# A ring of twelve weight slots in place of six for the experts of a two-block network on one Trainium2 core

## The reference, cut to what matters

```python
def moe_ffn(h, w_router, b_router, w_gate_up, b_gate_up, w_down, b_down):   # h: 256 x 1024
    logits = h @ w_router + b_router
    top_val, top_idx = lax.top_k(logits, 4)          # 4 of 32 experts for each token
    gates = jax.nn.softmax(top_val, axis=-1)
    ...
    def expert_block(args):
        xe, e = args
        gu = xe @ w_gate_up[e] + b_gate_up[e]        # 1024 x 2048
        g = jnp.minimum(gu[:, :1024], 7.0)
        u = jnp.clip(gu[:, 1024:], -7.0, 7.0)
        act = (u + 1.0) * (g * jax.nn.sigmoid(1.702 * g))
        return act @ w_down[e] + b_down[e]           # 1024 x 1024
    ...                                              # times its gate, summed over each token's experts
```

## Time and profile before

| | |
|---|---|
| Median of 3 runs | 2454.33 us (2451.05 to 2455.43) |
| The profiled execution, its own time | 2454.55 us |
| Its span, first to last instruction | 2452.9 us |
| TensorE busy, share of the span | 2257.8 us, 92% |
| VectorE, ScalarE, GpSimd busy | 1003.7, 623.0, 168.7 us |
| Bytes moved by DMA | 633.59 MB, mean 258 GB/s |
| Experts phase, from its first DMA (1438.97) to the last copy out of PSUM | about 998 us |

### The profile page before, as it was taken

How to read it: one execution, slowest core, us unless ns; L and a number is a source line. 1 busy time by engine, 2 the same in 40 slices (tenths; PEclk the granted TensorE clock), 3 DMA queues, 4 the chain that set the end, 5 groups by cost and what they waited for, 6 DMA issues and landing times. The chain is left out here.

```text
span 2452.9 us, 32053 instructions
## 1 busy us (share of the span) xinstructions
PE 2257.8 (92%) x12673; PEld 1398.2 (57%) x12674; DVE 1003.7 (41%) x1460; ACT 623.0 (25%) x848; POOL 168.7 (7%) x192
## 2 busy tenths in 40 slices
PE   7999989899999999989989989999999999999996
PEld 5886775688778777658868644333333333333332
DVE  4553582664466437556548641111111111111111
ACT  3432331443433322243426510000000000000000
POOL 4000020000000002000000000000000000000000
PEclk9999999999999999999999979999999999999999
DMA  8762312676287242158625349999999999999996
GB/s 281 260 234 79 112 64 69 230 255 219 72 301 243 73 158 78 37 181 279 227 82 161 117 165 371 418 418 418 418 418 411 404 404 411 407 405 399 404 403 248
DMA packets 231951, 633.59 MB, mean 258 GB/s; under 512 B 32472, under 2 KB 128744, under 8 KB 199056
## 3 DMA queue, kind: packets, MB, share of 16 engines
q1 hardware_dynamic: 231856, 632.24, 68.4%
HBM read 631.12 MB, written 1.07 MB: 258 GB/s over the span
## 5 line engine op out<-in xcount | busy, mean ns | idle before, releaser
L2511 PE MATMUL banks<-memory,attend_words 128*64 128x512 f32 x2048 | 481.1, 605 | 63.2 <-DMA memory<-in_w_gate_up 62.3
L365 PE MATMUL banks<-ffn_room 128*128 128x512 f32 x1920 | 454.4, 392 | 0.0
L365 PEld LDWEIGHTS banks<-ffn_room 128*128 128x128 f32 x1920 | 357.5, 188 | 73.6
L2511 PEld LDWEIGHTS banks<-memory,attend_words 128*64 128x64 f32 x2048 | 131.1, 136 | 388.1 <-issue 210.6
L2661 DVE TENSOR_TENSOR attend_words<-banks,memory 64x512 f32<-64x512 f32 x64 | 44.2, 690 | 738.4 <-PE banks L2511 738.0
L485 DVE TENSOR_TENSOR ffn_room<-memory,ffn_room 128x2048 fp32r<-128x2048 f32 x124 | 281.0, 2291 | 122.0 <-ACT ffn_room L442 122.0
L396 PE MATMUL banks<-ffn_room 128*128 128x512 f32 x1056 | 254.2, 397 | 17.4 <-DVE ffn_room L522 17.4
L442 ACT CAST ffn_room<-memory 128x2048 fp32r<-128x2048 f32 x124 | 232.7, 1906 | 106.9 <-PE banks L396 82.7
L396 PEld LDWEIGHTS banks<-ffn_room 128*128 128x128 f32 x1056 | 201.8, 192 | 66.2 <-DVE ffn_room L522 20.3
L2527 PE MATMUL banks<-memory,attend_words 128*64 128x512 f32 x1024 | 226.8, 594 | 0.0
L2527 PEld LDWEIGHTS banks<-memory,attend_words 128*64 128x64 f32 x1024 | 70.0, 135 | 130.9 <-issue 119.9
(11 more groups left out here) (419 smaller groups left out, 2108.4 us busy)
## 6 DMA issues: line engine op xcount, KB each, us to landing
memory<-in_w_gate_up SPq DMA_DIRECT2D x256, 1024.0 KB, 11.8
memory<-in_ffn_w SPq DMA_DIRECT2D x132, 1024.0 KB, 6.9
memory<-in_w_down SPq DMA_DIRECT2D x128, 1024.0 KB, 13.0
memory<-in_w_in SPq DMA_DIRECT2D x32, 1024.0 KB, 5.4
memory<-in_w_ada SPq DMA_DIRECT2D x32, 768.0 KB, 5.8
memory<-in_w_out SPq DMA_DIRECT2D x12, 1024.0 KB, 5.1
memory<-in_w_in SPq DMA_DIRECT2D x8, 800.0 KB, 4.6
memory<-in_ln_g SPq DMA_DIRECT2D x6, 512.0 KB, 3.9
```

Source lines behind the costliest of these rows:

```text
L365: m = nc.tensor.matmul(psum[:, GU + tt, :], x_parts[:, xp, k, tt * P:tt * P + P], rows, start=(n == 0), stop=(n == 3 * KD - 1))
L2511: m = mm(psum[halves[h], bank, :], room.xeT[:, k, :], rows[:, c0 + h * HALF:c0 + h * HALF + HALF], start=(k == 0), stop=(k == G8 - 1))
```

## The change

The ring's six slots stay as they are for all phases. For the experts six more places are added, each with a semaphore of its own (`chip.more`): slots 2 to 5 of `attend_later`, a new piece of `attend_words` (SLOT words more in `ATTEND_WORDS`), and `chip.xT`, which attention itself uses. Five of these (all but `chip.xT`) are loaded in the attention phase, right behind `b_down` on SP and ahead of the last four loads into the ring: chunks 6 and 7 of expert 0 and 0, 1, 2 of expert 1. The sixth place is loaded as the first load of the experts phase. From there on, each expert's 12 chunks have 12 fixed places, and a load waits for the chunk that was 12 before it in place of 6.

```diff
@@ class Chip
         *self.full, self.used = semaphores(nc, "ring", RING + 1)
+        self.more = semaphores(nc, "more", RING)
@@ class AttendRoom
         self.gatesT = w.take(chip.T)
+        self.more = [later[:, i * SLOT:i * SLOT + SLOT] for i in range(2, 6)] + [w.take(SLOT), chip.xT.rearrange("p k t -> p (k t)")]
@@ attend_phase, SP
             sp.dma_start(room.b_down[0:NE, :], b_down[0:1, :, :].rearrange("a e n -> (a e) n")).then_inc(s["mod"], 16)
+            for m in range(RING, 2 * RING - 1):
+                dst = room.more[m - RING]
+                sp.dma_start(dst, gate_up_rows(w_gate_up, *divmod(m, KD))).then_inc(chip.more[m - RING], 16)
             chip.issue(sp, loads, OUT + RING, OUT + N_OUT + RING)
@@ experts_phase
-    assert LOADS % RING == 0
+    CYCLE = 2 * RING
+    assert LOADS == CYCLE and CYCLE - G8 == D4
+    def place(e, j):
+        return j if first_turn(e) else (G8 + j) % CYCLE
     def slot(e, j):
-        return chip.slot(base + (j if first_turn(e) else G8 + j))
+        p = place(e, j)
+        return chip.ring[:, chip.slot(base + p), :] if p < RING else room.more[p - RING]
@@ experts_phase, SP
             def load(e, j, src):
-                sp.wait_ge(chip.used, taken(e, j - RING + 1))
+                sp.wait_ge(chip.used, taken(e, j - CYCLE + 1))
...
             def turn(e):
                 bias_row(e)
-                for k in range(G8):
-                    load(e, k, gu_rows(e, k))
+                for k in range(0 if not isinstance(e, int) else D4, G8):
+                    load(e, k, gate_up_rows(w_gate_up, e, k))
                 for k in range(D4):
                     load(e, G8 + k, down_rows(e - 1, k))
             bias_row(0)
-            for k in range(RING, G8):
-                load(0, k, gu_rows(0, k))
+            load(1, D4 - 1, gate_up_rows(w_gate_up, 1, D4 - 1))
             turn(1)
             with sp.Fori(2, NE) as e:
                 turn(e)
```

More of the change, by code:

```diff
@@ L1556, with gate_up_rows @@
 ALL = 2 * STEPS
+def gate_up_rows(w_gate_up, e, k):
+    return w_gate_up[0:1, ds1(e), k * P:k * P + P, :].rearrange("a e p n -> (a e p) n")
 def attend_loads(chip, w_in, w_out):
@@ L1604, in __init__, with attend_phase @@
         self.rows_rms = acc[:, 4 * WIDE:4 * WIDE + chip.T]
-ATTEND_WORDS = 6144 + 256 + 3 * WIDE + 4 * WIDE + 2048 + 4 * HD + P + 32 + 192 + 8 * NE + 2 * NE + 2 * P + 4 + 24 + 10 * NE
+ATTEND_WORDS = 6144 + 256 + SLOT + 3 * WIDE + 4 * WIDE + 2048 + 4 * HD + P + 32 + 192 + 8 * NE + 2 * NE + 2 * P + 4 + 24 + 10 * NE
 PIECES = ((0, P), (P, WIDE))
-def attend_phase(chip, s, routed, room, par, loads, base, n_project, b_down, mod_row):
+def attend_phase(chip, s, routed, room, par, loads, base, n_project, b_down, mod_row, w_gate_up):
     nc, D, KD, NT = chip.nc, chip.D, chip.KD, chip.NT
@@ L2390, with __init__ @@
 class ExpertRoom:
-    def __init__(self, chip, words):
+    def __init__(self, chip, words, attend):
+        self.more = attend.more
         w = Words(words, 0, EXPERT_WORDS)
@@ L2437, in slot, with filled @@
     def slot(e, j):
-        return chip.slot(base + (j if first_turn(e) else G8 + j))
+        p = place(e, j)
+        return chip.ring[:, chip.slot(base + p), :] if p < RING else room.more[p - RING]
     def full(e, j):
-        if first_turn(e):
-            return 16 * ((base + j) // RING + 1)
-        return e * (16 * LOADS // RING) + 16 * ((base + G8 + j) // RING + 1 - LOADS // RING)
+        p = place(e, j)
+        return chip.full[chip.slot(base + p)] if p < RING else chip.more[p - RING]
+    def filled(e, j):
+        p = place(e, j)
+        first = 16 * ((base + p) // RING + 1) if p < RING else 16
+        return first if first_turn(e) else e * 16 + (first + 16 * ((G8 + j) // CYCLE - 1))
     halves = [slice(CAP * h, CAP * h + CAP) for h in range(2)]
@@ L2461, in load @@
             def load(e, j, src):
-                sp.wait_ge(chip.used, taken(e, j - RING + 1))
-                dst = chip.ring[:, slot(e, j), :]
+                sp.wait_ge(chip.used, taken(e, j - CYCLE + 1))
+                dst = slot(e, j)
                 if len(src.shape) == 3:
                     dst = dst.rearrange("p (c n) -> p c n", c=2)
-                sp.dma_start(dst, src).then_inc(chip.full[slot(e, j)], 16)
+                sp.dma_start(dst, src).then_inc(full(e, j), 16)
             def turn(e):
                 bias_row(e)
-                for k in range(G8):
-                    load(e, k, gu_rows(e, k))
+                for k in range(0 if not isinstance(e, int) else D4, G8):
+                    load(e, k, gate_up_rows(w_gate_up, e, k))
                 for k in range(D4):
@@ L2506, in gate_up @@
                 for k in range(G8):
-                    pe.wait_ge(chip.full[slot(e, k)], full(e, k))
-                    rows = chip.ring[:, slot(e, k), :]
+                    pe.wait_ge(full(e, k), filled(e, k))
+                    rows = slot(e, k)
                     for bank, c0 in ((GATE_BANK, 0), (UP_BANK, D_EXPERT)):
@@ L2521, in down @@
                 for i in range(D4):
-                    pe.wait_ge(chip.full[slot(e, j0 + i)], full(e, j0 + i))
-                    rows = chip.ring[:, slot(e, j0 + i), :]
+                    pe.wait_ge(full(e, j0 + i), filled(e, j0 + i))
+                    rows = slot(e, j0 + i)
                     for c in range(2):
@@ L2832, in second_half @@
             room = AttendRoom(chip, parts, later, words, routed)
-            attend_phase(chip, s_attend, routed, room, par, loads, base, n_project, b_down, mod_row)
+            attend_phase(chip, s_attend, routed, room, par, loads, base, n_project, b_down, mod_row, w_gate_up)
             nc.all_engine_barrier(sems_to_clear=s_attend.span())
-            experts_phase(chip, s_first, base + n_project + N_OUT, routed, ExpertRoom(chip, words), room.gatesT, room.b_down,
+            experts_phase(chip, s_first, base + n_project + N_OUT, routed, ExpertRoom(chip, words, room), room.gatesT, room.b_down,
                           w_gate_up, b_gate_up, w_down)
```

2 lines of the change are left out of this document (removed).

## The result

The changed kernel took 2428.13 us (median of 4 runs, 2426.5 to 2430.2) against 2454.69 us of the kernel before (4 runs, 2451.05 to 2455.43). The ratio is 0.9891, with a 95% interval of 0.9879 to 0.9903. It is faster by 26.6 us where 13.4 were forecast, and the time lies 6 us under the lower end of the range.

What follows compares the result with a forecast made beforehand. The prediction took the DMA stream up to the last gate-up chunk, plus a TensorE tail, as the bound. 2454.55 - 15.5 (six loads fewer) + 2.1 (gap at 1473) = 2441.1 us; range 2434 to 2447.5 us, a little over 80%.

Steps and rivals of the forecast that it cites:

- What bounds the kernel: Experts phase: it ends when its last gate-up chunk has landed, plus a tail on TensorE; DMA 30.9 us a turn, TensorE 27.95.
- Six loads fewer, 15.5 us: From the gap at 1473 to the last gate-up chunk, 356 loads in place of 362: gain 6 x 2.576 = 15.5 us.
- The rate of the stream: Experts stream: the mean of 2.576 us a load was taken, since it goes over the whole stream.
- a rival of 4%: Experts stream meets the lower of two rate levels from the start: 2.628 us a load, 2459.6 us, slower than before; 4%.
- The prediction's own sign of being wrong: Wrong if the stretch's rate differs by over 1%, gaps show in later turns, or TensorE waits for down chunks at the end.
- the upper level all through: Experts stream: a longer queue keeps it at 418 GB/s, 2.509 us a load, 24 us more gain, about 2417 us; 4%.
- The gap at 1473: Idle DMA stays; SP's bias row there waits for GpSimd's spreading until 1479.01, delaying the next chunk's load: cost 2.1 us, once.
- The bias rows hold SP in later turns at no cost: Steady turns: SP is held up to 9 us a turn, but up to eleven queued loads (28 us) cover the DMA; cost nothing.
- Loads in attention, 0: Five loads made in attention, 12.9 us from about 1382, partly in idle DMA time; 0 to 0.3 us, taken as 0.
- The tail: After the last gate-up chunk, eight down loads take 20.6 us and just land in time; length kept, 0 to 0.3 us more.
- Waits: TensorE has no wait for gate-up chunks in the first seven or so turns after the gap, in place of one from 1541 on.

Runs made afterwards that it cites:

- e11: Kernel before with only expert 0's bias row loaded and used for all experts, the other 31 rows left out: 2434.01 us, 0.9918.
- e12: Changed kernel with only expert 0's bias row loaded and used for all experts: 2420.66 us, 0.9864 against the kernel before.
- e4: Changed kernel's twelve places, but each load waits for the chunk six before it and none is loaded in attention: 2455.06 us, 0.9998 against the kernel before.
- e8: Changed kernel's twelve places, but each load waits for the chunk seven before it, none loaded in attention: 2443.92 us, 0.9966 against the kernel before.
- e9: Changed kernel's twelve places, but each load waits for the chunk nine before it, none loaded in attention: 2435.02 us, 0.9921 against the kernel before.
- e3: Changed kernel with the five loads moved from attention to the start of the experts phase: 2429.8 us, 0.9890 against the kernel before.
- e10: Changed kernel plus a second 8 KB row loaded into partition 0 in each turn: 2446.5 us, 0.9969 against the kernel before.
- e15: Changed kernel, bias row in 16 separated pieces, plus a second row of 16 x 480 B into partition 32 each turn: 2446.64 us, 0.9967 against the kernel before.
- e14: Changed kernel, bias row in 16 separated pieces, plus a second row of 16 x 480 B into partition 36 each turn: 2429.34 us, 0.9895 against the kernel before.
- e16: Kernel before, bias row in 16 separated pieces, plus 15 rows of 8 KB into partitions 4 to 28 and 64 to 92 each turn: 2483.75 us, 1.0116.

## Why the prediction was too high, step by step

- **What bounds the kernel**: right. The end is the last gate-up chunk and a fixed tail, before and after.
- **Six loads fewer, 15.5 us**: right in its count, and in its worth where the rate is steady: with the gap's term it made the forecast's 13.4, and from e11 to e12, without rows, the six loads gave 13.4 us.
- **The rate of the stream**: this is the step that failed. "I take the mean, since it goes over the whole stream" held 2.576 us a load fixed on both sides. Counted from SP's first issue behind the gap to the last gate-up chunk, it was (2410.88 - 1477.38) / 362 = 2.579 before and (2386.61 - 1480.29) / 356 = 2.546 after. The sum over the profiled executions is 6 x 2.579 = 15.5, less 2.9 for the gap, plus 356 x 0.033 = 11.7: 24.3 us, the 24.27 seen at that chunk. The term forecast as 0 was 11.7 us. It is the fall from 418 to 404 GB/s, which the prediction had seen, called unexplained, and then put in a rival of 4%. What the runs showed in its place: the rate falls when a part of each load that the bias row holds back by 0.31 us a turn is some 5.9 us behind and the queue of six has next to nothing left for the others (e4, e8, e9, e11). The prediction's own sign of being wrong, a rate that differs by over 1%, came true: 416 GB/s against 409.
- **The rival "the upper level all through"**: it named the right cause (a longer queue) and was set aside because the engines looked full "at either level with about the same five loads queued". The share of busy DMA, 1.02 and 1.01, could not show it: it counts a packet that is held up as busy, and the late stretch has 16 us of that a turn. From "the DMA share is 1.01 throughout" the prediction took that no DMA engine had time left, and that reading was wrong. Nor did the count of queued loads say which part they were queued for. Its 2417 us was also too good: the level of 418 is the 15 fast parts', while TensorE waits for the slow one, at 30.43 us a turn and not 30.1.
- **The gap at 1473**: right in kind and in size. The spreading ended at 1479.55, not 1479.01, the row was issued at 1479.74 and the chunk at 1480.29, 2.9 us later than before. Of these, 0.9 us is that the whole phase began later in this execution (its first DMA at 1439.91 and not 1438.97; over all the profiled executions here it lies between 1432 and 1445), and 2.0 us is the wait forecast at 2.1.
- **The bias rows hold SP in later turns at no cost**: right. SP issues the row 0.2 us after the end of a spreading up to 1589 and 0.7 us or more after it in nearly all later turns, and the stream stays full. But I looked at the row's wait alone and not at its transfer, which was the larger cost.
- **Loads in attention, 0**: right, and e3 shows that they could as well be made later.
- **The tail**: right (41.8 us). **Waits**: none in the seven turns from 1464 to 1658, then in every turn, at most 0.6 us each; the forecast had seven turns or so.

What stays open: why the slowest part loses 0.7 us a turn when the fast parts run out of work once a turn, though it has loads queued itself. It was seen together each time (before, e4, e8, e10, e15), with the held-up packets, but not separated. Nor is it shown why twelve loads reach their limit at 11.4 us: from 5.9 us with six, at 2.5 us for each load more, it would be an estimated 21.

## What to carry to other kernels

Where a stream is full by the share of busy DMA and its rate still steps down with nothing else changed, look at the landing times of the 16 parts of one load before holding the rate constant: a small transfer into one partition in every turn sets one part back each time, the queue's length decides how long that stays hidden, and a longer queue then gives more than its extra loads. Take small one-partition rows out of the stream (load them all once, one to a partition), and compare the cost of the replacement on the engine that is next in line. Sending them to different partition groups helped only for rows cut in 16 pieces (e14); with whole rows it was not shown, and 15 of them made it worse (e16).

## What the hardware showed that I had not expected

- 8 KB into partition 0 sets one of 16 parts of a stream of 1 MB loads back by 0.31 us (2.79 us between landings in place of 2.48), and it never catches up while the stream is full; 16 pieces of 512 B did the same (0.35 us), though each engine then carries one.
- Six loads queued hold that off up to 5.9 us of distance, seven up to about 7.8, twelve up to about 11.4; past it the stream falls from 418 GB/s to between 399 and 411. With nine, 10.8 us were reached without a fall.
- A share of busy DMA of 1.01 says nothing of room left: some 65 packets a turn that were held up, by 16 us in sum, are in it, while the rate is 404 GB/s and not 418.
- A load issued to idle DMA engines has its first part down 4.4 us later. With twelve places the median gate-up load into a slot of the ring takes 22.1 us from issue to landing (11.8 before), and nothing is lost by that:

```profile
memory<-in_w_gate_up SPq DMA_DIRECT2D x161, 1024.0 KB, 22.1
```
